# A two-block transformer layer on one Trainium2 core: the second token tile's turn and split placed behind the first tile's query scores

## The reference, cut to what matters

```python
h = rms_norm_2(x, norm_ffn)                              # x: 256 tokens, 1024 wide
q = einsum('td,dhk->thk', h, w_query)                    # 8 heads x 2 sides x 128
s = einsum('thpk,hpnk->thpn', q, sub_keys)               # scores against 128 keys per side
top_s, top_i = top_k(s, 16)                              # per head and side
best_s, best_pos = top_k(all 16x16 sums of both sides, 16)
idx = the expert of each of the 16 best sums             # one of 16384
g = softmax(best_s)
act = gelu(einsum('td,thkd->thk', h, expert_u[idx]))
x = x + einsum('thk,thkd->td', g * act, expert_v[idx])
```

## Time and profile before

| what | us |
|---|---|
| median of 3 runs (all alike) | 1238.28 |
| the profiled execution's own time | 1239.19 |
| its span in the profile | 1237.0 |
| mean granted TensorE clock, share of full | 0.989 |
| PE / DVE / ACT / POOL busy | 1097.0 / 979.1 / 549.7 / 590.0 |
| q0, the gathers' queue: bytes | 268.45 MB |

### The profile page before, as it was taken

How to read it: one execution, slowest core, us unless ns; L and a number is a source line. 1 busy time by engine, 2 the same in 40 slices (tenths; PEclk the granted TensorE clock), 3 DMA queues, 4 the chain that set the end, 5 groups by cost and what they waited for, 6 DMA issues and landing times.

```text
span 1237.0 us, 13575 instructions
## 1 busy us (share of the span) xinstructions
PE 1097.0 (89%) x4676; PEld 724.1 (59%) x4676; DVE 979.1 (79%) x1960; ACT 549.7 (44%) x1070; POOL 590.0 (48%) x547
## 2 busy tenths in 40 slices
PE   6999999999999999999588887888879888787877
PEld 6988888788989889977244433444324443222322
DVE  6599999998887767686988777887778867877655
ACT  5665676654456444994433233323332233222311
POOL 0089999999840000010554545553545545444432
PEclk9999999999999999999799999999999999999999
DMA  6554434444464655336899999999999999999996
GB/s 248 193 182 170 171 137 139 155 149 165 176 214 160 225 188 179 132 137 255 358 427 426 428 427 428 426 427 426 426 427 427 427 427 427 427 427 410 427 427 275
DMA packets 53941, 374.23 MB, mean 303 GB/s; under 512 B 6896, under 2 KB 6896, under 8 KB 9200
## 3 DMA queue, kind: packets, MB, share of 16 engines
q0 software_dynamic: 37152, 268.45, 51.6%
q1 hardware_dynamic: 14512, 100.67, 22.8%
q10 hardware_dynamic: 2208, 4.24, 1.0%
HBM read 372.29 MB, written 1.05 MB: 302 GB/s over the span
## 4 chain that ended last, share of the span: by engine, by line
PE 44%; DMA 25%; DVE 24%; ACT 4%; issue 3%; POOL 0%; POOLq 0%; DVEq 0%; SPq 0%; ACTq 0%
DMA big<-in_experts,big 11%; PE unit L450 10%; PE unit L452 10%; PE unit L451 10%; PE unit L779 9%; DMA row<-in_experts,big 6%; DMA conv_in<-in_experts,big 4%; DVE w_lo L1589 3%; DVE row L2062 3%; DMA work_two<-in_experts,big 2%; DVE big L2062 2%; DVE big L1968 2%; DVE conv_acc L1612 2%; DVE big L1965 2%; DVE big L2072 1%
## 5 line engine op out<-in xcount | busy, mean ns | idle before, releaser
L1299 ACT ACTIVATE probs<-ident,big 128x128 f32<-128x128 f32 x255 | 102.4, 402 | 430.8 <-DVE big L2072 430.8
L779 PE MATMUL unit<-row,probs 128*128 128x512 f32 x448 | 215.4, 610 | 45.9 <-ACT probs L1299 45.7
L1589 DVE TENSOR_TENSOR w_lo<-w_raw,w_hi 128x2048 fp32r<-128x2048 f32 x89 | 207.6, 2339 | 50.3 <-ACT w_hi L907 50.3
L907 ACT CAST w_hi<-w_raw 128x2048 fp32r<-128x2048 f32 x89 | 169.4, 1905 | 87.3 <-DMA w_raw<-in_weights 45.8
L779 PE MATMUL unit<-big,probs 128*128 128x512 f32 x344 | 168.3, 620 | 39.3 <-ACT probs L1299 39.2
L2434 POOL DMA_INDIRECT row<-in_experts,big x112 | 134.2, 1198 | 128.6 <-PE unit L779 112.1
L450 PE MATMUL unit<-in_hi,w_hi 128*128 128x256 f32 x544 | 189.2, 348 | 1.6 <-DVE in_lo L1676 0.9
L450 PE MATMUL unit<-w_hi,in_hi 128*128 128x512 f32 x432 | 171.0, 396 | 0.7 <-ACT big L1044 0.7
L779 PEld LDWEIGHTS unit<-row,probs 128*128 128x128 f32 x448 | 78.3, 190 | 156.1 <-ACT probs L1299 97.2
L451 PE MATMUL unit<-w_hi,in_lo 128*128 128x512 f32 x432 | 168.3, 390 | 0.0
L452 PE MATMUL unit<-w_lo,in_hi 128*128 128x512 f32 x432 | 168.3, 390 | 0.0
(11 more groups left out here) (319 smaller groups left out, 1672.0 us busy)
## 6 DMA issues: line engine op xcount, KB each, us to landing
w_raw<-in_weights SPq DMA_DIRECT2D x90, 1024.0 KB, 4.8
w_waiting<-in_weights SPq DMA_DIRECT2D x2, 1024.0 KB, 9.1
row<-in_experts,big POOLq DMA_INDIRECT x112, 14.8
big<-in_experts,big POOLq DMA_INDIRECT x89, 13.4
big<-in_x SPq DMA_DIRECT2D x2, 512.0 KB, 5.1
big<-in_mem ACTq DMA_DIRECT2D x1, 1024.0 KB, 4.9
big<-in_x ACTq DMA_DIRECT2D x1, 1024.0 KB, 6.6
big<-in_sub_keys_t ACTq DMA_DIRECT2D x1, 1024.0 KB, 6.8
```

The source lines that it names most:

```text
L779: m = e.matmul(unit[:, half * 512:(half + 1) * 512], diag_places[g % 12], UV.ap(g)[:, D + half * 512:D + (half + 1) * 512], start=first, s ...
L907: e.copy(split.ap(p)[0][:, :, :], raw.ap(p)[:, :, :]).then_inc(*mark("hi", p))
L1299: e.activation(diag_places[g % 12], ident[:, :], ACT.Copy, scale=here).then_inc(*mark("diag", g))
L1589: e.tensor_tensor(lo_part[:, :, :], raw.ap(p)[:, :, :], hi_part[:, :, :].bitcast(F32), ALU.subtract).then_inc(*mark("lo", p))
```

## The change

On PE, the transposes of tile 1 move behind the scores of tile 0. On ACT, tile 1's hi parts move behind the score copy of tile 0, and the exponential of the first choice moves ahead of the score copy of tile 1 and of the hi part of FIRST_UNDER. On DVE, the lo part of pq0's second piece moves ahead of tile 1's residual addition; tile 1's lo parts move behind `normed_tile(0)`, between the two parts of the first choice; the first dot product moves ahead of the lo part of FIRST_UNDER. No instruction is added or removed.

```diff
@@ pe @@
             first_queries(0, 0)
-            turn_tile(1, 0)
             first_queries(1, 0)
             turn_queries(0)
             score(0, [0])
+            turn_tile(1, 0)
             first_queries(0, 1)
             first_queries(1, 1)
             turn_queries(1)
@@ act @@
             tile_root(0)
             tile_squares(1)
             tile_root(1)
-            turned_tile(1)
             first_queries_copy(0)
             turned_queries_copy(0)
             score_copies(0, [0])
+            turned_tile(1)
             first_queries_copy(1)
             turned_queries_copy(1)
+            choose_exp(0)
             score_copies(0, [1])
             hi(FIRST_UNDER)
-            choose_exp(0)
             table(GELU_TANH)
@@ dve @@
             turned_tile(0)
+            lo(piece("pq0", 1))
             add_out("sb", 1)
-            lo(piece("pq0", 1))
             tile_inverse(0)
             tile_inverse(1)
-            turned_tile(1)
             for _ in choose(0, (0,)):
                 pass
             normed_tile(0)
+            turned_tile(1)
             for _ in choose(0, (1,)):
                 pass
+            dot_product(0)
             lo(FIRST_UNDER)
-            dot_product(0)
```

## The result

The changed kernel takes 1243.34 us (median of 6 runs, 1242.98 to 1244.70), the kernel before beside it 1238.19 (6 runs, 1237.67 to 1238.28). The ratio is 1.0043, 95% interval 1.0032 to 1.0053: 5.15 us slower. The direction and the range were right; the move was forecast as 3.9, that is 1.2 us too small.

The account below looks back on a forecast made before the run. Bound: the full DMA gather stream over 256 picks. Loop 3.7 us late plus 2.5 for the clock is 6.2; 6.2 + 7.0 - 9.3 = +3.9 on 1238.28 gives 1242.2 us, range 1238.8 to 1244.2.

Parts of the forecast that it names:

- A late loop makes the end late: Start of the loop over the picks: 6.2 us late, moving the DMA stream and the end by +3.9 us.
- The early part: Ahead of the loop: first gather at 587.73, tile 1's lo parts at 588.55, PE's products of tile 1 at 589.65.
- The transposes cost nothing: PE, tile 1's transposes behind tile 0's scores: takes away nothing that tile 0 waited for.
- the 1.19 us: DVE, lo part of pq0's second piece ahead of the addition: choice and first gather 1.19 us earlier.
- The clock fell: PE, gap before tile 1's products: clock falls to half, 5.1 us of slow work costing 2.5 us more.
- the list behind the first copy: ACT, tile 1: second copy 1.33 behind the first, exponential 1.28 + 0.4, score copy 0.58, hi part 1.9 us.
- The cover: Gather queue at pick 32: lands 9.3 us after issue, 7.0 taken as its own, the difference hiding loop lateness.
- The small latencies of the rival: Lone gather landing in 4.8 us, move +1.7, 1240.0; by the skill's estimated 4.4 us, 1239.6; chance 0.14.
- The rival without cover: Gather of pick 32: its 9.3 us all its own, so the whole 6.2 us comes through, 1244.5; chance 0.08.
- Where the stream goes thin: Gather queue in the loop: runs thin in the tens, is overtaken about pick 32.
- The first wait of DVE for a row: DVE in the loop, 683.24 before: about 4 us later, or one of several earlier waits.

Follow-up runs that it names:

- g2: Kernel before, with the lo part of FIRST_UNDER computed three times more on DVE ahead of the loop; 1243.06 us, ratio 1.0039.
- g4: f4 with ACT's exponential of the first choice put ahead of its first copy of tile 1; 1236.86 us, ratio 0.9987.
- f4: Changed kernel with tile 1's transposes before tile 0's scores, its split half before the choice, FIRST_UNDER's hi part between ACT's copies; 1238.62 us.
- f1: Changed kernel with ACT's exponential of the first choice ahead of its copies of tile 1's queries; 1244.25 us, ratio 1.0053.
- f2: Changed kernel with exponential and gelu table load ahead of ACT's tile 1 copies, FIRST_UNDER's hi part between them; 1240.46 us, ratio 1.0018.
- f3: Changed kernel with 28 unread matmuls on PE in its gap ahead of tile 1's products; 1242.85 us, ratio 1.0038.
- h1: Kernel before with only the lo part of pq0's second piece moved ahead of tile 1's residual addition on DVE; 1238.82 us, ratio 1.0003.
- g1: Kernel before, with the lo part of FIRST_UNDER computed once more on DVE ahead of the loop; 1238.82 us, ratio 1.0001.
- g3: Changed kernel with tile 1's residual addition again ahead of the lo part of pq0's second piece; 1243.43 us, ratio 1.0044.

## Why the prediction was right, and where its size was off

**A late loop makes the end late: right.** After slice 22 no slice of the changed kernel's strip loses anything, and the medians of ten kernels keep to "first gather's move, or lateness less 2.3, whichever is larger" within 1 us: 4.9 for 5.15 measured, g2 4.7 for 4.62, g4 -1.1 for -1.58, f4 0.2 for 0.47. The furthest are f1, f2 and f3, each 0.8 to 1.0 above it. As a fit of times this holds; as a mechanism only the dependence on lateness is shown, and not the 2.3, as told below.

**The early part: right.** From the common point, with its 1.02 us taken off, the forecast gave the first gather at 586.71 (586.74 measured), tile 1's lo parts at 587.53 (587.56) and PE's products at 588.63 (588.74). The transposes cost nothing in their new place. The prediction credits the 1.19 us to the move of the lo part; h1 shows that this move alone makes the first gather 0.84 later, so the gain belongs to the two moves together.

**The clock fell: right; its price was 0.8 too high.** The stretches of 1 us:

```profile
585.00:586.00 1.00, 0.00 (x0) 0.00 (x0) 0.90 (x6) 0.00 (x0) 0.00 (x0) 0.67 0.00 0
...
592.00:593.00 1.00, 1.00 (x6) 0.84 (x5) 0.93 (x5) 0.00 (x0) 0.69 (x2) 0.92 1.01 361
```

PE's granted clock fell from 1.00 to 0.50 (2.4 to 1.2 GHz) during 585 to 586, 3 to 4 us after PE's last transposes ended (they start at 581.04 and last 1.04), and rose again at 592, 3.5 us after the products began. I had taken the 5.1 us of the earlier trace rows, so 2.5 us of cost. Half of 3.5 is 1.7, and f3 measures 1.6. The first copy should come at 597.9 - 1.0 = 596.9 and came at 596.10.

**The term that was too small is the list behind the first copy.** I priced it with the durations of before: second copy 1.33 behind the first, then 1.28 + 0.4, score copy without waiting, hi part. It took 2.62 instead of 1.33 to the second copy, and the scores, whose clock had fallen to 0.50 again while PE waited for that copy, took 2.08 instead of the 1.16 us that they need at full clock (f3), so that the score copy waited another 0.45. Less 0.8 from the clock, plus 1.3, plus about 0.5, the loop's lateness became 7.2 instead of 6.2. That one microsecond is nearly all of the miss of 1.2, if the prediction's own cover is kept.

**The cover: 2.3 fits the times, but partly by luck.** The prediction took 7.0 us as the latency of a gather with nothing ahead of it, and so a cover of 9.3 - 7.0 = 2.3. In the changed kernel the gather issued at 628.12 is followed by a stretch in which the engines run short (197 GB/s in 630 to 632), so that little stands ahead of it:

```profile
row<-in_experts,big POOLq DMA_INDIRECT x1, 7.0
```

It landed 7.0 us after its issue. But other traces have quicker ones. The first gather, on empty engines, landed after 6.5 to 6.7 us in g1, g2, g3, g4 and h1, where the prediction had reckoned 7.8 from the sixth; in g3 the tenth took 5.9. The first and the tenth gather of g3:

```profile
conv_in<-in_experts,big POOLq DMA_INDIRECT x1, 6.5
...
conv_in<-in_experts,big POOLq DMA_INDIRECT x1, 5.9
```

With 5.9 to 6.5 the same reckoning would give a cover of 2.8 to 3.4. Cover read from the medians is 2.1 in the changed kernel (7.2 - 5.15), 1.9 in g1 and 2.4 in g2. Cover read at the 64th row is 1.3 (7.2 - 5.9), 0.8 and 1.2. So a true cover of about 1 us and a late loss of 1.2 us, which the traced execution of before has and these three do not, add up to the 2.3. That the reckoning at pick 32 hit this sum is luck, as far as the traces tell. Why the queue covers only about 1 us, and how often the late loss occurs in executions that were not traced, stays open.

The small latencies of the rival, 4.8 as the weight loads have it, and 4.4, are seen for no gather. By the Trainium skill's page DMA: Bandwidth & Descriptors, section Anatomy of one DMA (SWDGE path), a transfer of 1 MB would take an estimated 4.4 us; the quickest gather whose landing the traces hold took 5.9, so the trace disagrees and decides. The rival without cover is contradicted by the times, 5.15 for a lateness of 7.2; at the 64th row the truth lies about halfway between it and the prediction's own 2.3.

**Where the stream goes thin: half right.** I had it thin in the tens and overtaken at pick 32. It is short from the tenth gather on, at 612, and stays so to 656. The loss was not one dry stretch at the end but many small ones. The first wait of DVE for a row was forecast about 4 us later than 683.24, or as several early ones. It came for the next row, at 691.10: from the common point 122.73, where before waits for the same row at 685.67, 116.28 behind. That is 6.4 later, more than the forecast move of the stream, 3.9, and than that of the end, 4.8.

## What to carry to other kernels

A transfer stream that is full from some moment on can be moved earlier only if everything that feeds it moves too. Write down two numbers before reordering its start: how much earlier the first transfer goes, and how much in hand the stream has behind it. The second can't be read from one row: reckoned at pick 32 it was 2.3 us here, and at the 64th row the traces show 0.8 to 1.3 for the change, g1 and g2. Read the stream at a place where the engine waits for a landed row in both kernels, and look whether the two executions lose time elsewhere as well. To find out whether a lateness explains a loss, put the same delay into the old kernel with nothing else changed: g2 answered with one small edit what the changed kernel's trace alone could not. And when a wait is the visible end of a list of work on another engine, taking that wait away does nothing until the list itself is shorter (f1), but is worth its whole length when it is the last one left (g4).

## What the runs showed that was not expected

ACT sometimes starts long after PE's last instruction before it has ended. In the kernel before, the second copy starts as the transposes end. In the changed kernel PE's transposes end at 596.74 + 0.66 = 597.40 and ACT's copy starts at 598.72, 1.3 us later; in f1 it is the second copy too, 1.6 us, in f2 the first copy, 1.4 us, in f3 the score copy, 2.7 us, and its releaser is given as remote. In g3 the second copy shows none. The changed kernel, f2 and g3 have the same list of instructions on PE, so it isn't tied to a place in that list. PE's ends are modelled and some of its records can be missing, and none of my runs varied this by itself. What it is stays open. Nor is it shown to be the reason for the wider scatter of some kernels: f4 scatters over 5.2 us and g3 over 3.3, and no such delay between PE and the copies stands in their traces.

The clock's return isn't a fixed time after work begins: it took 5.1 us in the kernel before. With the same products behind a gap of the same length (6.65 or 6.66 us) it took 2.9 in f1, 3.5 in the changed kernel, 4.9 in f2 and some 6 in g3. A cost that depends on it has a range, not a value.
